# The SSD scan of a hybrid mixer in two chunks, on one core

## What is computed

```
CHUNK = 128                      # 256 tokens: nc = 2 chunks; 2 groups of 8 heads, head dim 64, state 128
a_cum = cumsum(dt * A, within a chunk)
seg   = a_cum[l] - a_cum[s];  Lmat = exp(where(l >= s, seg, -inf))
cb    = einsum('bclgn,bcsgn->bclsg', Cc, Bc)
y_diag = einsum('bclsg,bclsgr,bcsgrp->bclgrp', cb, Lmat, xdt)
decay_states = exp(a_cum[last] - a_cum);  states = einsum('bclgn,bclgr,bclgrp->bcgrpn', Bc, decay_states, xdt)
prev  = states carried from chunk to chunk, times exp(a_cum[last])
y_off = einsum('bclgn,bcgrpn,bclgr->bclgrp', Cc, prev, exp(a_cum))
y = y_diag + y_off + d_skip * x;   then y * silu(z), a group norm, and w_out together with the MLA branch
```

## Time and profile before

| | |
|---|---|
| median of the runs | 1202.93 us |
| the profiled execution: its time, and its span | 1201.64 us, 1199.9 us |
| PE, DVE, ACT, POOL busy | 97%, 72%, 54%, 6% of the span |
| from the first decay matrix of the scan to the next weights' matmuls | 933.79 to 953.93 us |
| granted TensorE clock, mean | 0.997 |

### The profile page before, as it was taken

One profiled execution on the slowest core, in us unless ns is written; L12 is line 12 of the kernel. 1 busy time (PEld: TensorE's weight loads), 2 busy tenths in 40 slices (PEclk: granted clock), 3 DMA queues, 4 the chain that ended last, 5 costly groups with the idle time before them and its releaser, 6 DMA issues.

```text
span 1199.9 us, 17774 instructions
## 1 busy us (share of the span) xinstructions
PE 1167.5 (97%) x6763; PEld 1013.3 (84%) x6763; DVE 863.1 (72%) x1243; ACT 652.7 (54%) x883; POOL 73.5 (6%) x112
## 2 busy tenths in 40 slices
PE   8999999999999999999999999999999999999997
PEld 7898878888888887888878888888988888888886
DVE  6687788888767778888576765557986866655655
ACT  5546456555545555555466444446756755545443
POOL 9200011110000001110000000000000000000000
PEclk9999999999999999999999999999999999999999
DMA  7633699997464269998535655544651053655560
GB/s 252 228 113 123 230 340 329 319 306 259 149 195 129 71 215 336 328 315 276 201 116 176 211 185 200 176 159 149 194 194 52 22 197 124 211 185 190 168 219 36
DMA packets 143238, 236.33 MB, mean 197 GB/s; under 512 B 6357, under 2 KB 106950, under 8 KB 143174
## 3 DMA queue, kind: packets, MB, share of 16 engines
q1 hardware_dynamic: 130402, 196.73, 49.4%
q0 software_dynamic: 10400, 37.77, 8.5%
q10 hardware_dynamic: 2372, 0.96, 0.3%
HBM read 234.37 MB, written 1.05 MB: 196 GB/s over the span
## 4 chain that ended last, share of the span: by engine, by line
PE 87%; DVE 7%; ACT 3%; issue 2%; DMA 1%; POOL 0%; ACTq 0%; DVEq 0%; POOLq 0%
PE ps L2293 18%; PE ps L2047 10%; PE ps L2049 10%; PE ps L2051 10%; PE ps L2296 9%; PE ps L1937 3%; PE ps L1939 3%; PE ps L1938 3%; DVE wlo L1120 2%; PE ps L1984 2%; PE ps L1985 2%; PE ps L1986 2%; PE ps L2136 1%; PE ps L2138 1%; PE ps L2137 1%
## 5 line engine op out<-in xcount | busy, mean ns | idle before, releaser
L1120 DVE TENSOR_TENSOR wlo<-raw,whi 128x2048 fp32r<-128x2048 f32 (+2 forms) x185 | 414.6, 2256 | 131.0 <-ACT whi L626 130.6
L626 ACT ACTIVATE whi<-raw 128x2048 fp32r<-128x2048 f32 (+2 forms) x185 | 348.4, 1889 | 140.1 <-PE ps L2051 61.1
L2293 PE MATMUL ps<-a,whi 128*128 128x512 f32 x1024 | 255.9, 392 | 2.0 <-DVE wlo L1120 1.4
L2293 PEld LDWEIGHTS ps<-a,whi 128*128 128x128 f32 x1024 | 186.6, 188 | 38.5 <-issue 1.8
L2296 PEld LDWEIGHTS ps<-a,wlo 128*128 128x128 f32 x1024 | 139.7, 190 | 10.0
L2296 PE MATMUL ps<-a,wlo 128*128 128x256 f32 x1024 | 142.7, 282 | 0.0
L2047 PE MATMUL ps<-whi,hh 128*128 128x512 f32 x376 | 117.7, 394 | 5.0 <-DVE wlo L1120 5.0
L2049 PE MATMUL ps<-wlo,hh 128*128 128x512 f32 x376 | 116.6, 391 | 0.0
L2051 PE MATMUL ps<-whi,hl 128*128 128x512 f32 x376 | 116.4, 391 | 0.0
L2049 PEld LDWEIGHTS ps<-wlo,hh 128*128 128x128 f32 x376 | 71.0, 189 | 15.4
L2051 PEld LDWEIGHTS ps<-whi,hl 128*128 128x128 f32 x376 | 70.9, 188 | 15.1
(11 more groups left out here) (434 smaller groups left out, 1960.4 us busy)
## 6 DMA issues: line engine op xcount, KB each, us to landing
stage<-in_w_ada_dram POOLq DMA_DIRECT2D x72, 512.0 KB, 5.3
raw<-in_w_up_dram SPq DMA_DIRECT2D x32, 1024.0 KB, 7.5
raw<-in_w_down_dram SPq DMA_DIRECT2D x32, 1024.0 KB, 7.7
raw<-in_ffn_w_gate_dram SPq DMA_DIRECT2D x22, 1024.0 KB, 5.4
raw<-in_ffn_w_up_dram SPq DMA_DIRECT2D x22, 1024.0 KB, 5.4
raw<-in_ffn_w_down_dram SPq DMA_DIRECT2D x22, 1024.0 KB, 5.1
raw<-in_moba_w_qkv_dram SPq DMA_DIRECT2D x11, 1024.0 KB, 6.4
raw<-in_w_in_dram SPq DMA_DIRECT2D x10, 1024.0 KB, 5.3
```

The lines of the kernel that those rows point to most:

```text
L626: A.activation(whi[:, s, 0:size], raw[:, s, 0:size], ACT.Copy).then_inc(w_hi, 1)
L1120: V.tensor_tensor(wlo[:, s, 0:size], raw[:, s, 0:size], whi[:, s, 0:size].bitcast(F32), ALU.subtract).then_inc(w_lo, 1)
L2293: T.matmul(bank(b + m), wh[:, c, m * P:(m + 1) * P], a2[:, c].rearrange("p k n -> p (k n)"), start=(c == 0), stop=False)
```

## The change

The scan becomes two chunks. The per-head decay matrices lose the block across (256 columns are left: the two causal blocks). For the block across, the decay between key s of tile 0 and query l of tile 1 is split in a factor of s, exp(sum to the end of tile 0 minus sum to s), and one of l, exp(sum within tile 1):

- PE's running sums are now taken within a tile, and the tile's total at tile 0; DVE copies and subtracts two 16-column pieces into `sm[:, 2]` (`edge_arg`), ACT takes their exp (`edge_exp`).
- POOL multiplies `xdt` of tile 0 with the first factor (1024 columns, into `xde`).
- Behind head 6 PE makes one product per group, C B of the block across (still part of `cb`) with `xde`: two float32 matmuls of 512 columns into banks 2 and 3.
- Behind head 9 DVE multiplies them with the second factor as it reads PSUM (two operations of 512 columns, into `cross`).
- POOL adds `cross` to `xs` of tile 1 (1024 columns); DVE's `add_half` for that tile waits for this. The two `add_half` move from behind heads 10 and 12 to behind 11 and 13.

```diff
@@ POOL, after its last DMAs
+            pool.wait_ge(edge_exp, 1)
+            pool.wait_ge(xdt_done, 1)
+            G.tensor_tensor(xde.rearrange("p (h n) -> p h n", h=H), xdt[:, 0].rearrange("p (h n) -> p h n", h=H),
+                            sm[:, 3, 0:H].unsqueeze(2).to_broadcast([P, H, DH]), ALU.mult).then_inc(xde_done, 1)
+            pool.wait_ge(cross_done, 1)
+            G.tensor_tensor(xs[:, 1], xs[:, 1], cross, ALU.add).then_inc(cross_in, 1)
@@ ACT
-            A.activation(rowc[0:H], rowf[0:H], ACT.Copy).then_inc(crow_hi, 1)
+            A.activation(rowc[0:H, 0:S], rowf[0:H, 0:S], ACT.Copy).then_inc(crow_hi, 1)
+            act.wait_ge(edge_arg, 1)
+            A.activation(sm[:, 3], sm[:, 2], ACT.Exp).then_inc(edge_exp, 1)
@@ ACT, per head
-                A.activation(tb[:, b, 0:S], bank(b, S), ACT.Exp, bias=nac[:, 0, h:h + 1])
-                A.activation(tb[:, b, S:SEG], ps[:, b, S:SEG], ACT.Exp, bias=nac[:, 1, h:h + 1]).then_inc(dec_exp, 1)
+                A.activation(tb[:, b, 0:P], bank(b, P), ACT.Exp, bias=nac[:, 0, h:h + 1])
+                A.activation(tb[:, b, P:S], ps[:, b, P:S], ACT.Exp, bias=nac[:, 1, h:h + 1]).then_inc(dec_exp, 1)
@@ DVE, rows_lo
-                V.tensor_tensor(rowc[32:32 + H], rowf[0:H], rowc[0:H].bitcast(F32), ALU.subtract).then_inc(crow_done, 1)
+                V.tensor_tensor(rowc[32:32 + H, 0:S], rowf[0:H, 0:S], rowc[0:H, 0:S].bitcast(F32),
+                                ALU.subtract).then_inc(crow_done, 1)
@@ DVE, ahead of the norm's factor
-            V.tensor_copy(rowf[0:H, 0:S], ps[0:H, 3, 0:S])
-            V.tensor_copy(rowf[0:H, S:SEG], ps[0:H, 3, P:S]).then_inc(row_f, 1)
+            V.tensor_copy(rowf[0:H, 0:S], ps[0:H, 3, 0:S]).then_inc(row_f, 1)
             V.tensor_scalar(sm[:, 7], bank(2, TT * H), -1.0, None, ALU.mult).then_inc(ac_done, 1)
+            V.tensor_copy(sm[:, 2, H:2 * H], ps[:, 2, H:2 * H])
+            dve.wait_ge(ac_done, 1)
+            V.tensor_tensor(sm[:, 2, 0:H], ps[:, 2, 2 * H:3 * H], sm[:, 7, 0:H], ALU.add).then_inc(edge_arg, 1)
@@ DVE, per head
-                V.tensor_tensor(pb[:, h % 2], tb[:, h % 2], cb[:, h // CT], ALU.mult).then_inc(dec_m, 1)
+                V.tensor_tensor(pb[:, h % 2, 0:S].rearrange("p (k n) -> p k n", k=2),
+                                tb[:, h % 2, 0:S].rearrange("p (k n) -> p k n", k=2),
+                                outer_blocks(cb[:, h // CT]), ALU.mult).then_inc(dec_m, 1)
-                if h in (10, 12):
-                    if h == 10:
-                        dve.wait_ge(z_done, 1)
-                    add_half((h - 10) // 2, 0)
+                if h == 9:
+                    dve.wait_ge(edge_exp, 1)
+                    for gr in range(2):
+                        dve.wait_ge(cross_ps, gr + 1)
+                        ins = V.tensor_tensor(cross[:, 512 * gr:512 * gr + 512].rearrange("p (h n) -> p h n", h=CT),
+                                              bank(2 + gr).rearrange("p (h n) -> p h n", h=CT),
+                                              sm[:, 3, H + CT * gr:H + CT * gr + CT].unsqueeze(2).to_broadcast([P, CT, DH]),
+                                              ALU.mult)
+                    ins.then_inc(cross_done, 1)
+                if h == 11:
+                    dve.wait_ge(z_done, 1)
+                    add_half(0, 0)
+                if h == 13:
+                    dve.wait_ge(cross_in, 1)
+                    add_half(1, 0)
@@ PE, running sums
-            T.matmul(ps[:, 2, 0:H], cum[:, 0:P], a[:, 0], start=True, stop=True)
-            T.matmul(ps[:, 2, H:2 * H], cum[:, P:S], a[:, 0], start=True, stop=False)
-            T.matmul(ps[:, 2, H:2 * H], cum[:, 0:P], a[:, 1], start=False, stop=True)
-            T.matmul(ps[0:H, 3, 0:S], a[:, 0], cum[:], start=True, stop=False)
-            T.matmul(ps[0:H, 3, P:S], a[:, 1], cum[:, 0:P], start=False, stop=True).then_inc(ac_ps, 1)
+            T.matmul(ps[:, 2, 0:2 * H], cum[:, 0:P], sm[:, 6], start=True, stop=True)
+            T.matmul(ps[:, 2, 2 * H:3 * H], cum[:, P:S], a[:, 0], start=True, stop=True)
+            T.matmul(ps[0:H, 3, 0:P], a[:, 0], cum[:, 0:P], start=True, stop=True)
+            T.matmul(ps[0:H, 3, P:S], a[:, 1], cum[:, 0:P], start=True, stop=True).then_inc(ac_ps, 1)
@@ PE, decay_rows
-                o = bank(h % 2, SEG)
-                T.matmul(o, selr[:, h:h + 1].to_broadcast([P, P]), rowc[:], start=True, stop=False)
-                T.matmul(outer_blocks(o), identr[:], maskt[:].unsqueeze(1).to_broadcast([P, 2, P]), start=False,
-                         stop=True).then_inc(row_ps, 1)
+                o = bank(h % 2, S)
+                T.matmul(o, selr[:, h:h + 1].to_broadcast([P, P]), rowc[:, 0:S], start=True, stop=False)
+                T.matmul(o.rearrange("p (k n) -> p k n", k=2), identr[:], maskt[:].unsqueeze(1).to_broadcast([P, 2, P]),
+                         start=False, stop=True).then_inc(row_ps, 1)
@@ PE, per head
-                T.matmul(ps[:, Y_BANK[half][1], cols], m_[:, P:S], v[0], start=True, stop=False)
-                T.matmul(ps[:, Y_BANK[half][1], cols], m_[:, S:SEG], v[1], start=False, stop=True).then_inc(y_done, 1)
+                T.matmul(ps[:, Y_BANK[half][1], cols], m_[:, P:S], v[1], start=True, stop=True).then_inc(y_done, 1)
+                if h == 6:
+                    pe.wait_ge(in_ready, PAIR0["mla"] + 4)
+                    pe.wait_ge(xde_done, 1)
+                    for gr in range(2):
+                        T.matmul(bank(2 + gr), cb[:, gr, P:S], xde[:, 512 * gr:512 * gr + 512], start=True,
+                                 stop=True).then_inc(cross_ps, 1)
```

More of the change, by code:

```diff
@@ L189, in build @@
         vm = st[:, 6144:8192].rearrange("p (t n) -> p t n", t=TT)
+        xde = st[:, 6144:7168]
+        cross = st[:, 7168:8192]
         qtok = st[:, 8192:9728].rearrange("p (t n) -> p t n", t=TT)
@@ L322, in build @@
         xdt_done = sem("xdt_done")
+        edge_arg = sem("edge_arg")
+        edge_exp = sem("edge_exp")
+        xde_done = sem("xde_done")
+        cross_ps = sem("cross_ps")
+        cross_done = sem("cross_done")
+        cross_in = sem("cross_in")
         tail_act = sem("tail_act")
```

## The result

The changed kernel takes a median of 1208.80 us (6 runs, 1208.08 to 1208.94). The kernel before, run beside it, took 1202.78 us (6 runs, 1199.88 to 1203.13). The ratio is 1.0053, with a 95% interval of 1.0043 to 1.0063: **6.0 us slower**, where 2.7 was forecast, and 0.4 us above the upper end of the range. The medians given for the kernel before beside the experiments leave out three slow executions (1352.43, 1644.54 and 3671.93 us).

What follows compares the result with a forecast made beforehand. PE, busy 97% of the span, was taken as the bound. Scan -1.0, first POOL hold +2.0, second +1.7 gave +2.7 us on 1202.93: 1205.6 us (own range 1204.8 to 1206.5, chance 0.50; whole range 1201.8 to 1208.4).

Steps and rivals of the forecast that it cites:

- Steps 2 to 5: Scan from head 0 on: narrower heads save, products (1.8 us) and scalings (1.3) cost; with Step 1, scan ends 1.0 us earlier.
- Step 1: Scan start: `rowc`'s low part on DVE is 128 columns shorter, so PE starts 0.13 us earlier.
- Step 3: Behind head 6: the two group products take PE 1.80 us, with nothing to hide them.
- Step 6: Before the scan: POOL's first operation holds DVE's 2-column chain, delaying PE's first rows by 2.0 us.
- Step 7: Behind head 10's multiply: POOL's addition holds DVE, adding 1.7 us, taken between two cases of 2.0 and 1.4.
- the first of the two cases named there: POOL's addition gets in behind head 10's multiply and holds head 11's multiply: 2.0 us.
- The wait for `cross_in`: DVE's wait for POOL's addition, 2.6 us of DVE work after POOL's start: adds nothing while POOL takes less.
- the second case: Head 11's multiply slips through too, and POOL's addition holds the second part of `add_half`: 1.4 us.
- C: Rival: POOL takes 3.4 us per operation and holds DVE throughout: +5.5 us, 1208.4; chance 0.12.
- A: Rival: DVE is held only 0.25 us per POOL operation, whatever its size: -0.5 us, 1202.4; chance 0.20.
- B: Rival: only one of the two POOL operations hurts, or both by half: +1.0 us, 1203.9; chance 0.13.
- D: Rival: POOL is harmless and the group products fall in a gap of PE: -2.6 us, 1200.3; chance 0.05.

Runs made afterwards that it cites:

- second_small: The changed kernel with only the second POOL operation (the addition of `cross`) cut to 2 columns: 1203.66 us, 1.0020 of the kernel before.
- both_small: The changed kernel with both POOL operations cut from 1024 to 2 columns, all waits kept: 1204.17 us, 1.0010 of the kernel before.
- no_pool: The changed kernel without POOL, whole result: ACT scales `xdt` in 16 operations, DVE adds `cross`: 1206.97 us, 1.0033 of the kernel before.
- no_products: both_small with the two group products on PE cut from 512 to 2 columns each: 1205.78 us, 1.0028 of the kernel before.
- both_small_fill: both_small with two or four PE transposes of a constant as filling in nearly every head's turn: 1202.21 us, 0.9998 of the kernel before.
- warm: The changed kernel with 16 PE transposes of a constant behind head 10, where PE waits for head 11: 1208.01 us, 1.0050 of the kernel before.
- after_fill: The changed kernel, both POOL operations whole, with the filling transposes of both_small_fill: 1207.41 us, 1.0040 of the kernel before.
- pieces: The changed kernel with the first POOL operation cut to 2 columns and the second split into four of 256: 1207.28 us, 1.0040 of the kernel before.

## Why the prediction was wrong

Of its +2.7 us the parts on DVE and POOL stand; it lacks a term of about the same size as the holds.

- **Steps 2 to 5, the heads: right.** The table of second_small has every one of them within 0.15 us. From the first decay row to the first weights it takes 19.39 us where before took 953.93 - 933.79 = 20.14, so 0.75 less, 0.9 forecast; the one run of both_small at a mean clock of 0.998 is 1.0 us faster than before's. Step 1 (-0.13 for the shorter `rowc` operation) is seen as *a*'s 7.4 to 7.3.
- **Step 3, "nothing hides it": right.** The products take 1.94 us on PE, and head 9's multiply comes when it was forecast.
- **Step 6, the first hold: the place and the mechanism right, the term too large.** It was put at 2.0 us and measured 1.5 by the cuts (8.9 - 7.4), 1.59 at the operation (1.75 - 0.16). The cause is that POOL's operation takes 1.92 us, that DVE's had been issued 0.20 us behind its start, and that it would have taken 0.16 anyway.
- **Step 7, the second hold: a term too small.** 1.7 forecast, 2.05 measured (2.90 - 0.85). The addition went in behind head 10's multiply and held head 11's whole, the first of the two cases named there; the average with the second case was not needed. The wait for `cross_in` added nothing, as said: `add_half` for tile 1 starts at 955.70, 2.3 us behind POOL's end.
- **How the holds were sized was wrong, and their sum came out by luck (3.7 forecast, 3.5 measured).** The prediction read 0.25 us per 256 elements out of the earlier trace rows and scaled it. What the runs show here is another rule: the DVE operation that is held waits to the end of POOL's instruction, whatever is left of it. This is the rule that the prediction cited and set aside. The Trainium skill, page "SBUF — State Buffer", section "Who interferes with whom", says that the one that issues first has the shared ports for its whole instruction, and the trace of after agrees in both directions: 931.06 + 1.75 = 932.81 beside POOL's 932.78, and POOL waiting for head 10's multiply. Why the operation on one partition in the earlier trace rows took 0.84 us and held DVE for 0.25 was not tried and stays open.
- **The step that failed: that nothing but PE's work and its waits sets PE's time.** The sum has no term for the granted clock, and no reason is given for leaving it out. The prediction took every PE duration from rows at full clock, and asked what the change adds to PE's path. It didn't ask what the change takes out. From head 0 to 5 ACT is the bound, so fewer columns on PE mean more waits there (2.94 of 4 us busy for 3.49), and from head 10 on DVE is. PE does the same work more slowly at the lower clock: in after, the profile has 1.25 us of this loss inside the scan (22.5 less second_small's 19.2 less the hold of 2.05) and 1.6 behind it (48.5 - 46.9), 2.85 in all. By the medians it is 6.0 - (-1.0 + 3.5) = 3.5 us; this is what is left when the other terms are taken off, not a measurement of the clock alone. The filling, which keeps the clock up, is worth 3.5 us in no_pool, 2.0 in both_small and 1.4 in after itself, each net of its own cost.
- **The rivals.** C had nearly the right total (+5.5) from a wrong cause: POOL takes 1.92 us for 1024 columns, not 3.4. A, B and D, which put the holds at 0.25 us each, at half and at nothing, are refuted by *a* and *b* of both_small and second_small: each of the two operations costs 1.5 us or more. Not one rival had the clock in it, though its mean of 0.997 stood among the numbers of before.

What stays open: where in the scan the clock falls. In both_small it is at 942 and not again; in after, whose heads 1 to 4 have the same work, it holds there and falls at 952.9; second_small loses it only at 954. That it falls somewhere in nearly every execution of the change, and in none of the profiles with filling in nearly every head, is shown; which gap decides it in one execution is not.

## What to carry to other kernels

Before work is taken off TensorE in a stretch that another engine bounds, look at the granted clock there and at how busy TensorE will be afterwards: the matmuls behind it can take longer than what was saved (the group products took 3.45 us in place of 1.94), and the full clock of the kernel before gave no sign of how near it was to falling. GpSimd work on large SBUF tensors should be costed, until a trace says otherwise, as a stop of VectorE for what is left of each of its instructions (1.6 and 2.05 us here), and so be put where VectorE is idle; cutting it into four pieces lowered its price from 2.05 to 1.45 us. When two runs of a change disagree with its sum, compare their mean clocks first, and use a run at full clock to check the sum.

## What the hardware showed that was not expected

- **Taking work away made the kernel slower.** By the medians no_products does 1.8 us less on TensorE than both_small and takes 1.6 us more; both_small_fill does more and takes 2.0 us less.
- **The clock fell without a long idle time.** In both_small TensorE's waits between the first decay rows and 941.8 are of 0.21, 0.51 and 0.35 us; the view of its waits there lists them as

```profile
PE ps L2612 <- DVE work L1887: 1.1, 3, 0.5
```

  The Trainium skill, page "TensorE: Matmul & The Clock Gate", section "A second HAM failure mode: psum-queue depth-cycling", describes such a loss from frequent short idles between groups of matmuls; this trace agrees, while after and second_small, with the same heads, kept the clock at this place.
- **One filled gap was not enough, filling in nearly every head was, in the profiles.** 1.92 us of transposes in the longest gap (warm) left two falls in its profile; two to four of them in nearly every head's turn left none in the three profiles that have them. The mean clock of 0.994 in three of after_fill's five runs suggests that this doesn't hold in every execution.
- **The hold didn't depend on the size of VectorE's operation.** An operation on 2 columns was held for 1.59 us by one on 1024, and an addition that reads one input from PSUM was not held at all (0.68 us in pieces, in the middle of POOL's four).
